# Summing the prompt's expert rows on TensorE with weighted strips, in place of VectorE's sums into PSUM

## What is computed

```python
eidx = jnp.take_along_axis(cidx, fpos, axis=-1).reshape(n, PEER_HEADS * PEER_TOPK)
g = jax.nn.softmax(fs, axis=-1).reshape(n, PEER_HEADS * PEER_TOPK)
act = jax.nn.gelu(jnp.einsum('nkd,nd->nk', u[eidx], xb).astype(jnp.float32), approximate=False) * g
return jnp.einsum('nk,nkd->nd', act.astype(xb.dtype), v[eidx])
```

## Time and profile before

| | us |
|---|---|
| median of three runs (3770.48 to 3777.56) | 3772.29 |
| the profiled execution | 3774.4 |
| its span, from the first to the last instruction | 3772.6 |

### The profile page before, as it was taken

One profiled execution on the slowest core, in us unless ns is written; L12 is line 12 of the kernel. 1 busy time (PEld: TensorE's weight loads), 2 busy tenths in 40 slices (PEclk: granted clock), 3 DMA queues, 4 the chain that ended last, 5 costly groups with the idle time before them and its releaser, 6 DMA issues.

```text
span 3772.6 us, 51895 instructions
## 1 busy us (share of the span) xinstructions
PE 2592.6 (69%) x20591; PEld 1669.0 (44%) x20591; DVE 2376.7 (63%) x5572; ACT 657.9 (17%) x1772; POOL 1681.0 (45%) x1716
## 2 busy tenths in 40 slices
PE   7889778568886256655776877865878723665765
PEld 5669556457764232221543435654777520000000
DVE  1442388788677976545643326888876798767541
ACT  1321211232102122112111111213211121011000
POOL 2000323423443466655566524251335346777774
PEclk8899889679998677775888988985998865666568
DMA  8866567636797789996789977692559869999997
GB/s 323 323 219 226 124 242 252 250 108 194 302 360 258 250 294 341 355 336 243 269 279 366 378 289 193 213 341 81 183 206 385 299 262 348 409 409 409 409 409 283
DMA packets 345907, 1077.15 MB, mean 286 GB/s; under 512 B 29818, under 2 KB 34208, under 8 KB 345536
## 3 DMA queue, kind: packets, MB, share of 16 engines
q0 software_dynamic: 230464, 829.27, 60.8%
q1 hardware_dynamic: 115200, 244.55, 17.7%
HBM read 1070.03 MB, written 3.67 MB: 285 GB/s over the span
## 4 chain that ended last, share of the span: by engine, by line
PE 29%; DMA 25%; DVE 24%; POOL 10%; issue 8%; ACT 3%; DVEq 0%; SPq 0%; ACTq 0%; POOLq 0%
DMA arena<-in_peer_v,arena 18%; POOL arena L2089 9%; PE pair L598 6%; DVE arena L2146 5%; PE row_sum L2227 4%; DVE row_sum L2159 4%; DMA arena<-in_peer_u,arena 3%; PE pair L1617 2%; DMA ring<-in_w_in 2%; PE pair L1602 2%; PE pair L1310 1%; DVE arena L1919 1%; PE row_sum L398 1%; PE pair L1272 1%; PE pair L1632 1%
## 5 line engine op out<-in xcount | busy, mean ns | idle before, releaser
L2089 POOL DMA_INDIRECT arena<-in_peer_u,arena x768 | 775.3, 1009 | 962.0 <-DVE arena L2146 736.3
L2227 PE MATMUL row_sum<-arena 128*32 128x512 f32 x2048 | 716.6, 822 | 571.5 <-DMA arena<-in_peer_v,arena 389.0
L2089 POOL DMA_INDIRECT arena<-in_peer_v,arena x768 | 795.3, 1036 | 534.1 <-PE row_sum L2227 240.4
L2146 DVE CUSTOM_DVE_ANT_1 arena<-arena,hT 128x1024 f32<-128x1024 f32 x512 | 621.9, 1223 | 243.1 <-DMA arena<-in_peer_u,arena 237.6
L2227 PEld LDWEIGHTS row_sum<-arena 128*32 128x32 f32 x2048 | 92.6, 125 | 1096.5 <-DMA arena<-in_peer_v,arena 616.6
L598 PE MATMUL pair<-hT,ring 128*128 128x256 f32 (+1 forms) x2240 | 459.2, 369 | 123.9 <-DVE arena L624 66.5
L598 PEld LDWEIGHTS pair<-hT,ring 128*128 128x128 f32 x2240 | 395.6, 218 | 212.8 <-DVE arena L624 68.9
L2146 DVE CUSTOM_DVE_ANT_0 arena<-arena,pair 128x1024 f32<-128x1024 f32 x256 | 310.2, 1219 | 191.9 <-DMA arena<-in_peer_u,arena 190.6
L2159 DVE SCALAR_TENSOR_TENSOR row_sum<-arena,row_sum 128x1024 f32<-128x1024 f32 x254 | 326.9, 1287 | 53.2 <-DMA arena<-in_peer_v,arena 44.6
L1602 PE MATMUL pair<-hT,ring 128*128 128x256 f32 (+1 forms) x1280 | 250.4, 359 | 20.8 <-DMA ring<-in_w_in 20.8
L1602 PEld LDWEIGHTS pair<-hT,ring 128*128 128x128 f32 x1280 | 221.2, 207 | 69.3 <-issue 24.7
(11 more groups left out here) (349 smaller groups left out, 3900.2 us busy)
## 6 DMA issues: line engine op xcount, KB each, us to landing
ring<-in_w_in SPq DMA_DIRECT2D x52, 2048.0 KB, 16.9
ring<-in_w_mod SPq DMA_DIRECT2D x12, 2048.0 KB, 8.5
arena<-in_w_mod SPq DMA_DIRECT2D x12, 2048.0 KB, 10.5
ring<-in_w_br SPq DMA_DIRECT2D x11, 2048.0 KB, 14.7
arena<-in_w_in SPq DMA_DIRECT2D x8, 2048.0 KB, 8.2
ring<-in_w_out SPq DMA_DIRECT2D x7, 2048.0 KB, 13.9
ring<-in_peer_wq SPq DMA_DIRECT2D x7, 2048.0 KB, 8.9
arena<-in_peer_u,arena POOLq DMA_INDIRECT x768, 7.3
```

The lines of the kernel that those rows point to most:

```text
L2089: pool.indirect_dma_start(rowbuf[i % NB], None, v_rows if which else u_rows, bass.IndirectOffsetOnAxis(ap=offset, axis=0))\
L2146: nc.vector.tensor_tensor_reduce(row, row, tile_rows(t), 1.0, 0.0, ALU.mult, ALU.add, row_dot[t][:, k:k + 1]).then_inc(sem("u_used"), 1)
L2227: return nc.tensor.matmul(row_acc[c][32 * g:32 * g + 32, :], strip[n % 2][:, g, :], row[:, 512 * c:512 * (c + 1)], start=(n == 0), stop=(n ...
```

## The change

`ON_DVE` becomes false for the prompt as well. The counts of semaphore events and the riding table follow: the prompt's rows now take 172 steps and not 155, and the steps of the output and the query stage are set anew. Buffers, the first steps and the earlier stages of the table stay.

```diff
--- before.py
+++ after.py
@@ -154,8 +154,8 @@
 
     units = len(UNITS[tag])
     rows = P * nt
-    n.update({"chosen": units, "final_tops": units, "final_exp": units, "u_used": rows, "v_used": rows, "strip": rows // 4 * s,
-              "row_gelu": rows // GROUP, "row_w": rows // GROUP, "no_T": 4 * nt * s, "w_T": 4 * nt * s,
+    n.update({"chosen": units, "final_tops": units, "final_exp": units, "u_used": rows, "v_used": rows, "strip": rows // 4,
+              "row_gelu": rows // GROUP, "row_w": rows // GROUP, "no_T": 4 * nt, "w_T": 4 * nt,
               "peer_res": 2 * nt, "lnf_in": 32, "x_done": nt})
     return n
 
@@ -175,7 +175,7 @@
 RIDE = {"m": {"norm": (0, 5, 1), "proj": (5, 5, 39), "ret": (5, 11, 2), "prep": (11, 14, 3), "scan": (14, 26, 12),
               "gate": (26, 26, 24), "branch": (26, 26, 12), "out": (26, 26, 8), "query": (26, 26, 16)},
         "s": {"norm": (-9, -9, 1), "proj": (-9, 50, 39), "ret": (50, 56, 2), "prep": (56, 59, 3), "scan": (59, 84, 24),
-              "gate": (84, 114, 24), "branch": (114, 124, 12), "out": (124, 130, 8), "query": (130, 158, 16)},
+              "gate": (84, 114, 24), "branch": (114, 124, 12), "out": (124, 136, 8), "query": (136, 172, 16)},
         "p": {"norm": (0, 8, 1), "proj": (8, 130, 39), "ret": (130, 146, 2), "prep": (146, 160, 3), "scan": (160, 206, 12),
               "gate": (206, 251, 24), "branch": (251, 273, 12), "out": (273, 288, 8), "query": (288, 318, 16)}}
 
@@ -2034,7 +2034,7 @@
                 q, n = divmod(m, 32)
                 return 32 * q + 8 * (n % 4) + n // 4
 
-            ON_DVE = tag == "p"
+            ON_DVE = False
 
             def sum_at(t, m):
```

## The result

The changed kernel takes 3983.54 us (median of three runs, 3971.5 to 3988.71), the kernel before 3772.29. The ratio is 1.0534, with a 95% interval of 1.0502 to 1.0565: 211 us slower, where 58 were forecast and 3915 us was the upper end of the range. The sign was right and the size was not.

What follows compares the result with a forecast made beforehand. Neither TensorE nor VectorE was taken as the bound as a whole; engines and DMA take turns. Terms of +29 us per layer, +58 for two, on the profiled 3774.4 us gave 3832, stated as 3830; range 3762 to 3915 us.

Steps and rivals of the forecast that it cites:

- Projections: Sample mix's projections: at most 17 us return from VectorE, rows add 11, ScalarE 3; -3 us per layer, bounds -12 and +8.
- Retention and preparation: Nine steps: nine VectorE sums leave the path, a u-row wait shrinks, three rows join; -13 us per layer, bounds -18 and -5.
- Scan: Scan levels go from 4.33 to 4.2 us, saving 3; a ScalarE group adds 3.6; 0 per layer, bounds -6 and +15.
- Gate and branch: Gate and branch products: TensorE carries the v rows itself, +10 and +6; +16 us per layer, bounds +3 and +35.
- Output and norms: Output products and norms: nine rows on TensorE, fewer VectorE sums, one more ScalarE group; +3 us per layer, bounds -3 and +11.
- Queries, the tail: Rows between queries end them 18 us later, and VectorE's residual and norm follow uncovered; +26 us per layer, bounds +15 and +38.
- the six row buffers run short: Rival: late v rows hold up TensorE, each of the scan's 25 rows could wait; 55 us per layer, 3940 us; chance 0.18.
- The first rival: VectorE was the true bound: rows ahead of the gate fit TensorE's gaps, 151 us return against +90; 3713 us; chance 0.12.

Runs made afterwards that it cites:

- the run with early buffers: Changed kernel with both halves of a prompt row summed in one step, its buffer returned then, the second half in the next 32 partitions: 3896.09 us.
- quick transfers: Gathers of prompt v rows moving 256 of 1024 columns: kernel before 3733.47 us, changed kernel 3886.45 us, changed kernel with buffers given back at once 3880.75 us.

## Why the prediction was wrong in size

**The step that failed** is the sum's silence on waits: it priced the rows' time on TensorE (0.64 to 0.98 us, which held) and gave the waits for v rows and for strips, which now stand in TensorE's own queue, no term; late v rows stood only in a rival of 0.18, and there in the scan. The profile after has 41.0 us of the one and 13.3 us of the other per layer, and with the v buffers given back at once the table's stages are 42.1 us per layer shorter, 35.6 of them in the projections, gate and branch, and the queries.

**Projections (-3 forecast, +21.5 measured) failed most.** "At most 17 us come back": 9.1 did, the 6.0 on L598 and 3.1 of the waits for ScalarE (19.5 before, 16.4 after). "About 11 rows at 0.98 us, 11 us" was right for the rows at the full clock, yet TensorE's busy time grew by 15.5 us: behind each of the two waits for v rows the granted clock was 0.50, where a row lasts 1.92 and not 1.05 us. What had no term are new waits: 12.9 us for v rows (5.02 and 7.86), 2.6 for a strip, and 3.0 listed as issue at the first row. 11 + 18.5 - 9.1 = 20.4, and 24.9 with 15.5 in place of 11, against 21.5 measured, so the account is good to some 3 us. The stage had a DMA share of 0.90, and I read that row for VectorE's busy time and not for when rows arrive. TensorE's timeline of the changed kernel at three of these waits:

```profile
677.90 1.92 PE L2227 MATMUL row_sum<-arena 128*32 128x512 f32 x4 [5.02 <-DMA arena<-in_peer_v,arena]
...
687.67 1.71 PE L2227 MATMUL row_sum<-arena 128*32 128x512 f32 x4 [2.56 <-DVE arena L2170]
...
704.02 1.92 PE L2227 MATMUL row_sum<-arena 128*32 128x512 f32 x4 [7.86 <-DMA arena<-in_peer_v,arena]
```

The clock in the stretch behind the first of them and behind the last:

```profile
677.90:680.00 2.10, 2.10 (x5) 0.43 (x6) 0.00 (x0) 0.00 (x0) 0.00 (x0) 0.50 1.05 411
704.02:705.90 1.88, 1.88 (x5) 0.22 (x5) 0.00 (x0) 0.00 (x0) 0.00 (x0) 0.50 1.03 415
```

**Retention and preparation (-13, measured -17.4)** held, at its favourable end (-18): VectorE was busy for 90.6 and TensorE for 49.1 of its 110 us, and there the change does what was hoped of it.

**Scan (0, measured +10.3).** A level is 4.16 us where 4.2 was forecast, as TensorE's timeline of the changed kernel shows for the earlier trace rows:

```profile
814.65 1.15 PE L1310 MATMUL pair<-arena 64*64 64x64 f32 x32
...
818.81 1.15 PE L1310 MATMUL pair<-arena 64*64 64x64 f32 x32
...
822.97 1.15 PE L1310 MATMUL pair<-arena 64*64 64x64 f32 x32
```

It is the sum of 3.2 and 0.98 with nothing between them (to 0.02 us). The rule that I had weighed in the prediction, a drain at a change of tiling mode (TensorEngine Tiling (Array Packing) in the Trainium skill, Key Properties), would have put it at 4.5; if there is a drain, the price of a lone row holds it already. The step that failed is "a level lasts 4.33 us" before, "3 us over 20 levels". The levels come in four series, and the first two of each had been shorter, without a wait for VectorE. TensorE's timeline of the kernel before at the first of them:

```profile
804.82 1.15 PE L1310 MATMUL pair<-const,arena 64*64 64x64 f32 x32 [0.79 <-issue]
807.64 1.15 PE L1310 MATMUL pair<-arena 64*64 64x64 f32 x32
```

2.82 and 3.3 us there, 3.95 and 4.16 after: (1.13 + 0.86) x 4 = 8 us. One level also waits 4.1 us for ScalarE behind the group of copies, as forecast (3.6), while the later levels give some 3 us back. With row matmuls over 64 columns the scan took 163.8 us, so here it is TensorE's time that counts.

**Gate and branch (+16, measured +31.8).** "89.7 + 30 x 0.98 = 119 us" is right for an engine that never waits, and it is what the run with early buffers shows, 119.3 us; with the branch 174.6 in all, +18.1. The other 14 us are the ring: 12.1 us of waits for v rows in the gate products, a DMA share of 0.90 where it had been 0.99.

**Output and norms (+3, measured +21.6).** I counted VectorE's sums that go and not its strips that come, and so not where they stand. One strip behind the norms costs 10.8 us of TensorE's time and the lower clock behind it; the run with fewer rows in that place shortened the stage by 23.1 us, more than its 21.6, though 12.3 of them only moved to the queries.

**Queries, the tail (+26, measured +33.0)** was right in mechanism and near in size: 81.3 us from the first query to the next norm where 75 was forecast, the residual behind TensorE's last half row as described. The queries and transposes end 26.4 us later where 18 were forecast, and the uncovered residual and norm add 6.6 where 8.4 were. With buffers at once the stretch is +19.9: 8.4 of the 13.1 us between the two are rows that come late, and 4.7 are the half row that no longer stands behind the transposes.

**The rivals.** The second one, "the six row buffers run short", is what happened, with a mechanism that was right ("a late v row now holds up the mix", "a v buffer given back one step later") in a place that was wrong. I put it into the scan, where the waits were 1.8 us, because the sum was easy to do there, and gave it no more than 0.18 because the scan's DMA share was 0.56. Most of the waits sit in stages whose share was higher: 12.9 us in the projections (0.90), 12.1 in the gate products (0.99), 6.2 in the queries (0.77). Its price, forecast as 110 us, was 70 to 79 for the late return, and it came on top of the forecast's terms. What was missed beside it shows in the column with buffers at once, which stands 29.7 us per layer over the forecast of +29: 15.7 in the projections, 15.6 in output and norms (the strip), 7.7 in the scan (the short levels) and 2.1 in gate and branch, less 5.3 in retention and preparation and 6.1 in the queries. The first rival was wrong: its two conditions, levels of 3.5 us and all 17 us of the projections, came out as 4.16 and 9.1. VectorE's sums were 151 us of the chain and little came back, because the transfers and TensorE took their place.

What isn't settled: how the remaining 66 us per layer of the run with buffers at once (132 over the kernel before, two layers) split between TensorE's time and its waits, what the lower clock behind the waits costs in all, and what the circle of the three queues in the projections costs, since no run breaks it. The narrow matmuls and the removed copies overlap with the other cures, so their 62 and 23 us aren't shares of the whole.

## What to carry to other kernels

Before moving a consumer of transfers to another engine, ask what else stands in that engine's queue. VectorE could wait for late v rows beside TensorE's work (24.0 us in the first sample mix, where quick transfers gave the whole kernel 33 us), and TensorE couldn't, since the mix itself stands behind each row. With the same bytes and the same buffers the ring is then too short, and one buffer fewer tells it: 22 us for the kernel before, 88 to 100 us for the changed one. Every helper of the moved step, here a strip of 0.29 us, also gets a place in a queue, and what stands ahead of it is part of its price.

When an experiment gives no gain, look at the price of its own edit before dropping the theory: returning the buffers early looked useless at +14 us, and the same edit gave 79 to 88 once the matmuls ran side by side again.

## What was unexpected of the hardware

Two 128x32 products of 512 columns in different columns of TensorE take 0.98 us as a pair among other products, and 1.84 us when both use the same columns. The order of the halves was therefore worth 0.86 us for a row that stands alone. A change of shape from 64x64 to 128x32 and back within each level of the scan cost nothing beyond the row itself, 4.16 us against 3.2 + 0.98. And TensorE's waits for single rows had a price behind them: after idle stretches of 5.0, 7.9 and 10.8 us the granted clock was 0.50, and a lone row lasted 1.92 us and not 1.05.
